# A two-block network step on one core: the conformer's layer-norm end one step later, and the turned ranks behind the LSTM's running sums

## The chip, the cores and the metric

The kernel runs on 1 core of one Trainium2 chip. The metric is the device time of one execution in microseconds; the time of a kernel is the median of its runs. A run is one launch that holds the whole computation. The profile is of one execution, and its times (us from the start of the span) come from the hardware profiler.

## The reference, cut to what matters

The model takes 256 tokens of width 1024 through a first block of two layers and a second block of one. Everything is float32.

```python
for l in range(2):                                  # first block
    proj = rms_norm(x, norm_g[l]) @ w_in[l]         # 1024 x 4376
    y_nsa  = sparse attention of q, k, v            # 8 heads of 64
    y_lru  = rg_lru(u_lru, ...)                     # gates, decay, scan over time
    u = ga * sigmoid(gb)                            # conformer branch
    u = depthwise conv of 31 taps (u)
    un = (u - mean(u)) * rsqrt(var(u) + eps) * ln_g + ln_b
    y_conv = silu(un) @ w_pw2                       # 512 x 512
    x = x + concat(y_nsa*silu(z), y_lru*silu(z), y_conv*silu(z)) @ w_out[l]
# second block: two mixers side by side, on 256 latent and 256 context tokens
cq  = rmsnorm(h @ w[:, 0:256],   g_cq)              # latent attention: ranks 256 and 128
ckv = rmsnorm(h @ w[:, 256:384], g_ckv)
q, k, v = cq @ w_uq, ckv @ w_ukv ...                # 4 heads, RMS-normed per head
i, f = gates;  F = cumsum(log_sigmoid(f));  M = cummax(i - F)   # mLSTM, both directions
x = x + gate * (concat(attention, mlstm) @ w_out)
x = x + gate * peer(h2)                             # 8 x 16 of 16384 experts for each token
```

## The kernel before, in words

The program is written out by hand, engine by engine. Each of TensorE (PE), VectorE (DVE), ScalarE (ACT), GpSimd (POOL) and SyncE (SP) has its own list of instructions and works through it strictly in order; semaphores named by events (`tell=...`, `at(...)`) tie the lists together. Matmuls write into PSUM banks. `take` hands them out in a fixed rotation, and TensorE waits there until the bank's previous content has been copied out (`taken`, `emptied`). SP loads weights, 2 MB at a time, into buffers that TensorE has finished with.

**First block, per layer.** After the projections a loop of 20 steps runs the attention. In each step TensorE makes scores of later heads, then what `BETWEEN` lists for that step, then turns (transposes) the weights of one head and multiplies them with the values. The steps around the change: in step 7 `BETWEEN` has `zn(1)`, a gate's projection; in step 8 `ada(0)`; in step 9 `mod(0)`, `pw(0)` and `pw(2)`, the two halves of the conformer's pointwise product; from step 10 on the output products `out12`. `pw` waits for the event `conv_act_ready`, which VectorE's `conv_act` gives (L1286). Ahead of that stand `layer_norm_end` (L1278: one multiply over 128x1024, four scale-and-add over 128x256, event `conv_normed`), and then on ScalarE the Tanh (L1531, event `conv_tanh`). `lru_scan` (L1248) and `lru_mixed` (L1259) are VectorE's work for the other branch; `lru_mixed` is first wanted in step 10. In VectorE's list the order is: scores of step 7, `layer_norm_end`, `z_nsa(1)`, `lru_scan`, `conv_act`, `lru_mixed`, scores of step 9.

**Second block, start ("head stage").** TensorE's list in `mix_tensor` (L1656): `mla` products, `conv_input` 4, 5, 0, 1, 2 (inputs of the mLSTM's convolution), the turns of `cq` and `ckv` (8 transposes into two banks, `cqT` and `ckvT`), `conv_input(3)`, the turns of the gates (`gate_i`, `gate_f`), the products `v(0)` and `v(1)`, a wait until VectorE has copied `ckvT` out, and then `queries(0)` (product `uq`), `v(2)`, `keys_values(0)` (`ukv`), and `heads_turned(0)`, which waits for `heads_normed`. After it six further rounds of `ukv` or `uq` products, turns of normed heads and a filling product follow.

VectorE's list in `mix_vector` (L1953): clear `qk_lat`, norm the ranks, `taken(0)` (copy `conv_input(0)` out), a polynomial for log(1+z) of the gates (event `log_gates_ready`), copy out `cqT` and `ckvT` with their gains (L2048 to L2053), `taken(1..3)`, four rounds of `silu` and `convolve`, copies of the gates, the running sums `sums(0)`, `sums(1)` up to the event `E_sum` (L2089), and then `head_norm(0)` (L2091). ScalarE's list (L2283 on): `values(0)`, `values(1)`, copies of `uq`, four squares (`head_squares`), then Exp of E, which waits for `E_sum`, then the square root for `head_norm(0)`.

**Rest.** After the head stage come attention and mLSTM of the first 128 tokens, their output product and the routing of the first expert head; from then on (about 706 us) GpSimd fetches expert rows of 8 KB, VectorE takes the dot products, TensorE sums them, and the other 128 tokens' mixers are fitted in between.

Of the kernel before, what the change touches and what calls it, by code (L numbers as in the profile page):

```python
# [252 lines left out]
class Banks:  # L253
# [32 lines left out]
    def filled(self, *key):  # L286
        return (f"bank{self.where(key)}_filled", *key)
# [736 lines left out]
def first_vector(c, m, block, K, x, l):  # L1024
# [261 lines left out]
    def conv_act():  # L1286
        dve.wait_ge(*at("conv_tanh", l))
        dve.stt(act, act, 1.0, conv, ADD, MUL, tell=("conv_act_ready", l))
# [18 lines left out]
    def between(step):  # L1307
# [4 lines left out]
        if step == 7:  # L1312
            layer_norm_end()
# [32 lines left out]
        if step == 8:  # L1346
            conv_act()
            lru_mixed()
# [37 lines left out]
def first_scalar(c, m, block, x, l):  # L1386
# [95 lines left out]
    def between(step):  # L1482
# [31 lines left out]
        if step == 4:  # L1514
            lru_decay()

    for step in range(STEPS):
# [11 lines left out]
        if step == 7:  # L1529
            act.wait_ge(*at("conv_normed", l))  # L1530
            act.f(m["conv_act"], conv, ACT.Tanh, scale=0.5, tell=("conv_tanh", l))  # L1531
# [124 lines left out]
def mix_tensor(c, m, K):  # L1656
# [48 lines left out]
    for o in range(3):  # L1705
        conv_input(o)
    pe.wait_ge(*at("ranks_normed", 0))
    bank = take("cqT")
    for k in range(2):
        for i in range(NT):  # L1710
            pe.turn(bank[:, k * T + i * P:k * T + i * P + P], m["cq"][:, i, k * P:k * P + P], ident,
                    tell=filled("cqT") if (k, i) == (1, NT - 1) else None)
    bank = take("ckvT")
    for i in range(TILES):
        pe.turn(bank[:, i * P:i * P + P], m["ckv"][:, i, 0:P], ident, tell=filled("ckvT") if i == TILES - 1 else None)
    conv_input(3)
# [9 lines left out]
    pe.wait_ge(*c.taken("ckvT"))  # L1726
# [226 lines left out]
def mix_vector(c, m, K, x):  # L1953
# [69 lines left out]
    dve.fill(qk_lat, 0.0)  # L2023
# [13 lines left out]
    taken(0)  # L2037
# [10 lines left out]
    dve.wait_ge(*full("cqT"))  # L2048
    for k in range(2):
        dve.ts(m["cqT"][:, k, :], tile("cqT")[:, k * T:k * T + T], vec[:, R_GCQ + k:R_GCQ + k + 1], MUL,  # L2050
               tell=emptied("cqT") if k else None)
    dve.wait_ge(*full("ckvT"))
    dve.ts(m["ckvT"], tile("ckvT")[:, :], vec[:, R_GKV:R_GKV + 1], MUL, tell=emptied("ckvT"))  # L2053
    for o in range(1, 4):
        taken(o)
    for o in range(4):
        silu((4, 5, 0, 1)[o])
        convolve(o)
# [30 lines left out]
    dve.tt(E, F, M, ADD, tell=("E_sum", 0))  # L2089

# [167 lines left out]
def mix_scalar(c, m, K, x):  # L2258
# [30 lines left out]
    values(1)  # L2289
    def product(n):  # L2290
# [17 lines left out]
    def head_norm(n):  # L2308
# [6 lines left out]
        if n == 0:  # L2315
            act.wait_ge(*at("E_sum", 0))
            act.f(m["E"], m["E"], ACT.Exp, scale=-1.0, tell=("E_ready", 0))
# [819 lines left out]
```

## Time and profile before

| | |
|---|---|
| time, median of 3 runs | 1426.55 us (1425.18 to 1427.67) |
| profiled execution: its own time | 1425.18 us |
| profiled execution: span | 1423.6 us, 1.6 us lie around it |
| TensorE busy | 1023.0 us, 72% |
| VectorE busy | 921.9 us, 65% |
| ScalarE busy | 357.7 us, 25% |
| mean granted TensorE clock | 0.842 of full speed |
| HBM read | 387.89 MB, 273 GB/s over the span |

Busy time is an average over stages with different limits: where one engine ends last in a stage, the others' busy share says nothing. In the rows further down, a number in square brackets is the time for which the engine was idle ahead of the instruction, with the engine and instruction that ended this.

### The profile page before, as it was taken

The numbers are of one execution on the slowest core, as the hardware profiler recorded it, in microseconds if no ns is written. First come the engines' busy times: TensorE is split into PE (matmuls) and PEld (weight loads), VectorE is DVE, ScalarE is ACT, GpSimd is POOL, SyncE is SP. The second block draws the span as 40 slices with busy tenths as digits, with TensorE's granted clock in tenths as the row PEclk, the third lists the DMA queues.
The fourth block names the chain that finished last, engine by engine and source line by source line (L and its number), as shares of the span: only waits on it lengthen the run. The fifth ranks groups of instructions, "written<-read, shape, count | busy, mean of one in ns | idle before, by whom it ended". The sixth has DMA issues, their size and how long they took to land.

```text
span 1423.6 us, 17219 instructions
## 1 busy us (share of the span) xinstructions
PE 1023.0 (72%) x6241; PEld 594.2 (42%) x6241; DVE 921.9 (65%) x2443; ACT 357.7 (25%) x813; POOL 288.0 (20%) x265
## 2 busy tenths in 40 slices
PE   7997999999899999978868668664543354543434
PEld 4776656577665556436534323332211122211111
DVE  5488633448864437544366788778777676777765
ACT  2013523101443412455244532321011110001100
POOL 0000000000000000000033334545433444433441
PEclk9998999999899899999979888976756666665765
DMA  8462562455456242162179899999999999999996
GB/s 295 150 193 98 187 220 89 162 178 165 144 182 222 63 144 96 59 239 90 34 290 412 327 420 418 418 414 419 415 421 415 419 414 416 417 414 414 420 421 274
DMA packets 111926, 391.10 MB, mean 275 GB/s; under 512 B 10971, under 2 KB 39182, under 8 KB 79586
## 3 DMA queue, kind: packets, MB, share of 16 engines
q0 software_dynamic: 37440, 268.45, 45.8%
q1 hardware_dynamic: 74402, 121.56, 24.7%
q8 instruction: 49, 0.80, 0.2%
q14 instruction: 35, 0.29, 0.1%
HBM read 387.89 MB, written 1.05 MB: 273 GB/s over the span
## 4 chain that ended last, share of the span: by engine, by line
DMA 21%; DVE 18%; PE 14%; ACT 4%; POOL 3%; issue 3%; DVEq 0%; ACTq 0%
DMA e_uv<-in_experts_dram,e_listed 21%; PE bank L169 13%; DVE e_uv L2814 5%; POOL e_uv L3021 3%; ACT m_W L229 1%; DVE e_rest L2745 1%; DVE e_diag L185 1%; ACT L229 1%; PE bank L174 1%; DVE e_hot L185 1%; DVE e_si L2743 1%; DVE e_si L2749 1%; DVE e_sv L2747 1%; DVE e_sv L2741 1%; DVE m_W L185 1%
## 5 line engine op out<-in xcount | busy, mean ns | idle before, releaser
L3021 POOL DMA_INDIRECT e_uv<-in_experts_dram,e_listed x252 | 278.9, 1107 | 1098.8 <-DVE e_listed L202 823.0
L169 PE MATMUL bank<-e_uv,e_diag 128*32 128x512 f32 x1024 | 232.1, 884 | 321.6 <-DVE e_diag L185 321.6
L2814 DVE CUSTOM_DVE_ANT_0 e_uv<-e_uv,e_h2q 128x1024 f32<-128x1024 f32 x192 | 229.3, 1221 | 84.5 <-DMA e_uv<-in_experts_dram,e_listed 84.1
L169 PEld LDWEIGHTS bank<-e_uv,e_diag 128*32 128x32 f32 x1024 | 41.5, 139 | 445.9 <-DVE e_diag L185 363.7
L169 PE MATMUL bank<-hT,weights 128*128 128x256 f32 x640 | 145.1, 388 | 2.7 <-DVE hT L191 1.4
L169 PEld LDWEIGHTS bank<-hT,weights 128*128 128x128 f32 x640 | 123.6, 195 | 22.3 <-issue 1.9
L229 ACT ACTIVATE e_act<-e_dot 128x4 f32<-128x4 f32 (+1 forms) x81 | 16.6, 205 | 394.7 <-DVE e_dot L2814 393.9
L229 ACT ACT_TABLE_LOAD x81 | 103.9, 1283 | 10.8 <-DVE e_dot L2814 2.8
L169 PE MATMUL bank<-weights,hT 128*128 128x512 f32 (+1 forms) x256 | 101.5, 552 | 2.2 <-DMA weights<-in_w_in_dram 2.2
L197 DVE SCALAR_TENSOR_TENSOR conv<-ubuf,vec,conv 128x256 f32<-128x256 f32 x240 | 96.8, 480 | 0.6
L2814 DVE CUSTOM_DVE_ANT_0 e_uv<-e_uv,e_hT 128x1024 f32<-128x1024 f32 x64 | 76.3, 1220 | 20.6 <-DMA e_uv<-in_experts_dram,e_listed 20.6
L169 PE MATMUL bank<-weights,mixT 128*128 128x512 f32 x192 | 87.5, 610 | 2.0 <-DVE mixT L202 1.6
L169 PEld LDWEIGHTS bank<-weights,hT 128*128 128x128 f32 x256 | 48.4, 192 | 49.1 <-issue 43.4
L169 PEld LDWEIGHTS bank<-e_hT,e_w_pq 128*128 128x128 f32 x512 | 63.8, 206 | 6.8 <-issue 6.0
L169 PE MATMUL bank<-e_hT,e_w_pq 128*128 128x128 f32 x512 | 65.4, 290 | 1.4 <-ACT e_hT L229 1.4
L169 PEld LDWEIGHTS bank<-weights,mixT 128*128 128x128 f32 x192 | 36.5, 196 | 46.3 <-issue 43.8
L185 DVE TENSOR_TENSOR x_sb<-bank,x_sb 128x512 f32<-128x512 f32 x16 | 11.1, 691 | 64.5 <-PE bank L169 64.5
L229 ACT ACTIVATE S<-S,mx 128x128 f32<-128x128 f32 (+1 forms) x64 | 29.1, 455 | 61.6 <-DVE mx L222 59.3
L169 PE MATMUL bank<-m_w,e_hT 128*128 128x464 f32 (+1 forms) x96 | 39.9, 570 | 1.2 <-PEq L3092 1.1
L185 DVE TENSOR_TENSOR e_w<-e_act,e_weight 128x4 f32<-128x4 f32 (+1 forms) x81 | 13.1, 162 | 30.9 <-ACT e_act L229 25.5
L197 DVE SCALAR_TENSOR_TENSOR ubuf<-fb,bank 128x512 f32<-128x512 f32 x4 | 2.7, 687 | 41.8 <-PE bank L169 41.8
L169 PE MATMUL bank<-m_wo,e_hT 128*128 128x512 f32 x64 | 28.2, 595 | 1.4 <-DVE m_qk_lat L202 1.4
(384 smaller groups left out, 1414.1 us busy)
## 6 DMA issues: line engine op xcount, KB each, us to landing
weights<-in_w_in_dram SPq DMA_DIRECT2D x16, 2048.0 KB, 8.1
weights<-in_w_ada_dram SPq DMA_DIRECT2D x8, 2048.0 KB, 8.7
weights<-in_w_out_dram SPq DMA_DIRECT2D x6, 2048.0 KB, 7.8
e_w_pq<-in_w_pq_dram SPq DMA_DIRECT2D x12, 1024.0 KB, 26.3
weights<-in_cmp_w_dram SPq DMA_DIRECT2D x4, 2048.0 KB, 8.4
m_w<-in_w_in_dram SPq DMA_DIRECT2D x2, 2048.0 KB, 8.1
m_wo<-in_w_ada_dram SPq DMA_DIRECT2D x2, 2048.0 KB, 8.4
m_w<-in_w_ada_dram SPq DMA_DIRECT2D x2, 2048.0 KB, 10.2
```

Of the source, the lines that this page charges most:

```text
L169: ins = self.engine.matmul(out, lhsT, rhs, start=start, stop=stop, **kw)
L174: ins = self.engine.transpose(out, a, ident)
L185: return self.mark(self.engine.tensor_tensor(out, a, b, op), tell)
L197: return self.mark(self.engine.scalar_tensor_tensor(out, a, s, b, op0, op1), tell)
L229: return self.mark(self.engine.activation(out, a, func, **kw), tell)
L2741: dve.mark(c.nc.vector.max(out_v[:, 0:8], values))
L2743: dve.mark(c.nc.vector.max_index(out_i[:, 0:8], out_v[:, 0:8], values))
L2745: dve.mark(c.nc.vector.match_replace(scratch, out_v[:, 0:8], values, -3e38))
L2747: dve.mark(c.nc.vector.max(out_v[:, 8:16], scratch))
L2749: return dve.mark(c.nc.vector.max_index(out_i[:, 8:16], out_v[:, 8:16], scratch))
L2814: dve.mark(c.nc.vector.tensor_tensor_reduce(u, u, h2q[tt][n], 1.0, 0.0, MUL, ADD, m["dot"][:, j:j + 1]), ("dots_set", g, c0) if n == c1 - ...
L3021: ins = c.nc.gpsimd.indirect_dma_start(out=to, out_offset=None, in_=rows, in_offset=bass.IndirectOffsetOnAxis(ap=of, axis=0))
```

## The change

It has two parts. In the first block, in both layers, `layer_norm_end` leaves step 7 and comes in step 8, behind `z_nsa(1)` and `lru_scan`; `lru_mixed` is put between it and `conv_act`; on ScalarE the Tanh moves from the end of step 7 into step 8, ahead of that step's copy of a turned head. In the second block the turns of `cq` and `ckv` move behind `v(1)` on TensorE and are spread over six banks instead of two; VectorE copies them out in eight pieces of 128x128 behind `E_sum`; the clearing of `qk_lat` and `taken(0)` move behind `log_gates_ready`, and the takings are interleaved with the convolutions; ScalarE makes Exp of E ahead of its first copy of `uq`.

```diff
--- before.py
+++ after.py
@@ -1309,8 +1309,6 @@
             conv_taps(*TAPS_AT[step])
         if step == 4:
             conv_taps(*TAPS_AT[step][0])
-        if step == 7:
-            layer_norm_end()
         for kind, *a in BETWEEN.get(step, ()):
             if kind == "zn":
                 z_nsa(*a)
@@ -1344,8 +1342,9 @@
         if step == 7:
             lru_scan()
         if step == 8:
+            layer_norm_end()
+            lru_mixed()
             conv_act()
-            lru_mixed()
 
     for step in range(STEPS):
         if step < len(UNITS):
@@ -1513,6 +1512,9 @@
                 modulation(*a)
         if step == 4:
             lru_decay()
+        if step == 8:
+            act.wait_ge(*at("conv_normed", l))
+            act.f(m["conv_act"], conv, ACT.Tanh, scale=0.5, tell=("conv_tanh", l))
 
     for step in range(STEPS):
         if step < len(UNITS):
@@ -1526,9 +1528,6 @@
         if 1 <= step <= len(UNITS):
             kind, qt, i, g = UNITS[step - 1]
             turned(step - 1, 2 * (qt + 1) * P if kind == "head" else P)
-        if step == 7:
-            act.wait_ge(*at("conv_normed", l))
-            act.f(m["conv_act"], conv, ACT.Tanh, scale=0.5, tell=("conv_tanh", l))
         if l + 1 < DEPTH and step == X_NORMED_AT:
             squares(l + 1, 0)
             root(l + 1, 0)
@@ -1702,18 +1701,8 @@
     conv_input(5)
     pe.wait_ge(*c.taken("blockT", "lat", NT - 1, 1))
     by_token("mla", TILES - 1, TILES - 1, B_QK + 16)
-    for o in range(3):
+    for o in range(4):
         conv_input(o)
-    pe.wait_ge(*at("ranks_normed", 0))
-    bank = take("cqT")
-    for k in range(2):
-        for i in range(NT):
-            pe.turn(bank[:, k * T + i * P:k * T + i * P + P], m["cq"][:, i, k * P:k * P + P], ident,
-                    tell=filled("cqT") if (k, i) == (1, NT - 1) else None)
-    bank = take("ckvT")
-    for i in range(TILES):
-        pe.turn(bank[:, i * P:i * P + P], m["ckv"][:, i, 0:P], ident, tell=filled("ckvT") if i == TILES - 1 else None)
-    conv_input(3)
     for a, name in enumerate(("gate_i", "gate_f")):
         bank = take(name)
         pe.wait_ge(*at("log_gates_ready", 0))
@@ -1723,7 +1712,16 @@
     by_token("v", 0, 0, 512)
     by_token("v", 1, 1, 512)
 
-    pe.wait_ge(*c.taken("ckvT"))
+    pe.wait_ge(*at("ranks_normed", 0))
+    for i in range(NT):
+        bank = take("cqT", i)
+        for k in range(2):
+            pe.turn(bank[:, k * P:k * P + P], m["cq"][:, i, k * P:k * P + P], ident,
+                    tell=filled("cqT", i) if k else None)
+    for i in range(TILES):
+        bank = take("ckvT", i)
+        pe.turn(bank[:, 0:P], m["ckv"][:, i, 0:P], ident, tell=filled("ckvT", i))
+    pe.wait_ge(*c.taken("ckvT", TILES - 1))
 
     def queries(i):
         view, landed = mix_weight(m, "uq")
@@ -2020,7 +2018,6 @@
     for name in ("M", "F"):
         dve.fill(m[name], 0.0)
 
-    dve.fill(qk_lat, 0.0)
     tmp = m["tmp"]
     f = gates[:, :, 8:16]
     dve.stt(tmp[:, 0], f, -1.0, f, MUL, MAX, tell=("gates_abs", 0))
@@ -2034,7 +2031,6 @@
             dve.ts(src[:, i, 0:width], src[:, i, 0:width], inv[:, i:i + 1], MUL,
                    tell=("ranks_normed", 0) if (name, i) == ("ckv", TILES - 1) else None)
 
-    taken(0)
     dve.wait_ge(*at("gates_exp", 0))
     log1p_unit(dve, tmp[:, 2], tmp[:, 1], tmp[:, 3], tmp[:, 4], tmp[:, 5])
     dve.ts(f, f, 0.0, MIN)
@@ -2045,15 +2041,9 @@
         dve.tt(both[1][:, :, of], f[:, :, d * ML_H:(d + 1) * ML_H], tmp[:, 2, :, d * ML_H:(d + 1) * ML_H], SUB,
                tell=("log_gates_ready", 0) if d else None)
 
-    dve.wait_ge(*full("cqT"))
-    for k in range(2):
-        dve.ts(m["cqT"][:, k, :], tile("cqT")[:, k * T:k * T + T], vec[:, R_GCQ + k:R_GCQ + k + 1], MUL,
-               tell=emptied("cqT") if k else None)
-    dve.wait_ge(*full("ckvT"))
-    dve.ts(m["ckvT"], tile("ckvT")[:, :], vec[:, R_GKV:R_GKV + 1], MUL, tell=emptied("ckvT"))
-    for o in range(1, 4):
+    dve.fill(qk_lat, 0.0)
+    for o in range(4):
         taken(o)
-    for o in range(4):
         silu((4, 5, 0, 1)[o])
         convolve(o)
     silu(2)
@@ -2087,6 +2077,16 @@
     sums(0)
     sums(1)
     dve.tt(E, F, M, ADD, tell=("E_sum", 0))
+
+    for i in range(NT):
+        dve.wait_ge(*full("cqT", i))
+        for k in range(2):
+            dve.ts(m["cqT"][:, k, i * P:i * P + P], tile("cqT", i)[:, k * P:k * P + P],
+                   vec[:, R_GCQ + k:R_GCQ + k + 1], MUL, tell=emptied("cqT", i) if k else None)
+    for i in range(TILES):
+        dve.wait_ge(*full("ckvT", i))
+        dve.ts(m["ckvT"][:, i * P:i * P + P], tile("ckvT", i)[:, 0:P], vec[:, R_GKV:R_GKV + 1], MUL,
+               tell=emptied("ckvT", i))
 
     def head_norm(n, g, rope_tile):
         heads, r1, r2 = m["both"][n % 2], m["r1"], m["r2"]
@@ -2287,6 +2287,9 @@
 
     values(0)
     values(1)
+    act.wait_ge(*at("E_sum", 0))
+    act.f(m["E"], m["E"], ACT.Exp, scale=-1.0, tell=("E_ready", 0))
+
     def product(n):
         kind, i, _ = HEAD_WORK[n]
         heads = m["both"][n % 2]
@@ -2312,9 +2315,6 @@
         for h in range(MLA_H):
             act.f(m["sq4"][:, h, :], heads[:, h, :], ACT.Square, accum_out=small[:, 24 + h:25 + h],
                   tell=("head_squares", n) if h == MLA_H - 1 else None)
-        if n == 0:
-            act.wait_ge(*at("E_sum", 0))
-            act.f(m["E"], m["E"], ACT.Exp, scale=-1.0, tell=("E_ready", 0))
         act.wait_ge(*at("head_inverse", n))
         act.f(small[:, 32:36], small[:, 28:32], ACT.Sqrt, tell=("head_root", n))
 
```

## Rows read from the trace of the kernel before

**Rows 1.** Windows: gather stage; us, then busy us (count) of PE, PEld, DVE, ACT, POOL, clock, DMA.

```profile
706.00:1423.00 717.00, 379.33 (x3344) 174.06 (x3343) 531.72 (x1396) 142.62 (x319) 287.75 (x261) 0.72 0.98 397
```

**Rows 2.** Timeline of PE, layer 0: start, us, what, count, [idle before].

```profile
174.40 1.05 PE L169 MATMUL bank<-constants,cond_mod_rows 128*128 128x2 f32 x8 [0.36 <-ACT cond_mod_rows L233]
176.22 7.14 PE L169 MATMUL bank<-xn,weights 128*128 128x256 f32 x32 [0.76 <-DVE xn L197]
```

**Rows 3.** Windows of PE alone, layer 0 from the pointwise product on.

```profile
176.20:234.00 57.80, 57.56 (x295) 1.00 0.55 191
```

**Rows 4.** Timeline of DVE, steps 7 and 8 of layer 0.

```profile
168.83 1.23 DVE L185 TENSOR_TENSOR conv<-conv,yt 128x1024 f32<-128x1024 f32 x1
170.09 1.38 DVE L192 TENSOR_SCALAR conv<-conv,vec 128x256 f32<-128x256 f32 x4
171.58 0.69 DVE L197 SCALAR_TENSOR_TENSOR zn<-zn,bank 128x512 f32<-128x512 f32 x1
172.30 2.44 DVE L218 TENSOR_TENSOR_SCAN fc<-fa,fd 128x256 f32<-128x256 f32 x4
174.85 1.23 DVE L197 SCALAR_TENSOR_TENSOR xn<-xn,conv 128x1024 f32<-128x1024 f32 x1
176.11 1.22 DVE L197 SCALAR_TENSOR_TENSOR mixT<-fb,fc 128x1024 f32<-128x1024 f32 x1
```

**Rows 5.** Timeline of ACT, layer 0: two Tanh.

```profile
169.44 0.60 ACT L229 ACTIVATE zn<-bank 128x512 f32<-128x512 f32 x1 [0.43 <-PE bank L169]
...
171.51 1.06 ACT L229 ACTIVATE xn<-conv 128x1024 f32<-128x1024 f32 x1 [1.10 <-DVE conv L192]
```

**Rows 6.** Timeline of PE, layer 1: the same pointwise product.

```profile
421.45 7.14 PE L169 MATMUL bank<-xn,weights 128*128 128x256 f32 x32 [0.76 <-DVE xn L197]
```

**Rows 7.** Timeline of PE, head stage.

```profile
551.97 1.04 PE L174 MATMUL bank<-constants,e_w_pq 128*128 128x128 f32 x8
...
559.31 14.00 PE L169 MATMUL bank<-m_wo,e_hT 128*128 128x512 f32 x32 [1.37 <-DVE m_qk_lat L202]
573.14 2.74 PE L169 MATMUL bank<-m_w,m_ctx 128*128 128x384 f32 x8
...
585.90 0.63 PE L174 MATMUL bank<-constants,e_w_pq 128*128 128x128 f32 x4 [1.43 <-DVE e_w_pq L185]
```

**Rows 8.** Timeline of DVE, head stage.

```profile
544.76 0.92 DVE L213 MEMSET m_qk_lat<- 128x1032 f32 x1 [0.16 <-issue]
...
549.04 1.25 DVE L191 TENSOR_SCALAR e_w_pq<-e_w_pq,m_small 128x128 f32<-128x128 f32 x4 [0.27 <-ACT m_small L229]
...
556.86 1.86 DVE L191 TENSOR_SCALAR m_ctx<-bank,cond_vec 128x256 f32<-128x256 f32 x3
...
578.89 0.68 DVE L185 TENSOR_TENSOR m_xn<-m_xn,m_M 36x512 f32<-36x512 f32 x1
...
581.85 0.96 DVE L185 TENSOR_TENSOR e_w_pq<-e_w_pq,m_small 128x768 f32<-128x768 f32 x1 [1.78 <-ACT m_small L229]
```

**Rows 9.** Timeline of ACT, head stage: last of the four squares, table load.

```profile
578.17 0.19 ACT L229 ACTIVATION_READ_ACCUMULATOR e_h2q<-e_w_pq 128x1 f32 x1
...
580.31 1.28 ACT L229 ACT_TABLE_LOAD   x1
```

**Rows 10.** Window of PE alone, head stage behind the first turned heads.

```profile
585.90:621.80 35.90, 35.90 (x138) 1.00 0.34 120
```

**Rows 11.** Timeline of PE, layer 0: one product behind a rest, and one without.

```profile
129.98 0.62 PE L169 MATMUL bank<-hidT,w 128*64 128x16 f32 x8 [3.70 <-DVE hidT L197]
130.73 8.95 PE L169 MATMUL bank<-hT,weights 128*128 128x256 f32 x32
...
140.53 7.12 PE L169 MATMUL bank<-hT,weights 128*128 128x256 f32 x32
```

**Rows 12.** Window of PE alone: the clock there.

```profile
130.00:134.40 4.40, 4.27 (x17) 0.50 0.00 2
```

**Rows 13.** Timeline of PE: the first levels of the first tile.

```profile
641.13 0.68 PE L169 MATMUL bank<-m_M,constants 36*128 36x128 f32 x4 [0.81 <-ACT cond_mod_rows L233]
```

## The prediction

> **What bounds the kernel now.** I read the page's forty slices first: from about 706 us on the DMA engines are full, before that they are not. The window over this gather stage [rows 1] shows it: DMA share 0.98, TensorE busy 379 of 717 us. Nothing of the change lies there, and its first transfer waits for the first routed expert list, the end of all that stands before. So I take the gather stage as a block that starts as much later as the work ahead of it ends later. Ahead of 706 us I asked, stretch by stretch, whether TensorE waits and for whom, with the timeline of one engine at a time. Behind the pointwise product of layer 0 it is busy 57.56 of 57.80 us [rows 3], behind the first turned heads of the head stage 35.90 of 35.90 [rows 10]. Whatever makes TensorE later at the start of such a stretch arrives whole at its end. At the two places that the change touches, TensorE already waits a little for VectorE: 0.76 us ahead of the pointwise product in each layer [rows 2, 6], 1.43 us ahead of the first turned heads [rows 7]. There VectorE's list is what ends last, and the change rewrites just this list.
>
> **Part 1, the layer-norm end, twice.** Before, VectorE does norm end, `z_nsa`, scan, `conv_act`, and the pointwise product starts 0.14 us behind `conv_act` [rows 2, 4]. The Tanh between norm end and `conv_act` (1.06 us [rows 5]) costs nothing: `z_nsa` and the scan (0.69 and 2.44 us [rows 4]) cover it. After, step by step:
> - The scores of step 7 end at 168.8 as before. `z_nsa` is now first and waits for its own Tanh, which ends at 170.04 [rows 5]. It runs from 170.1 to 170.8. Before, the norm end filled this hole; 1.3 us of it are now lost.
> - Scan, with its gaps, to 173.4.
> - Norm end: 168.83 to 171.55 before, 2.72 us with gaps [rows 4], so to 176.1.
> - Tanh on ScalarE 176.1 to 177.2. The cover is now `lru_mixed`, 1.22 us [rows 4], which ends at 177.35: it hides the Tanh, but it also stands ahead of `conv_act`.
> - `conv_act` from 177.4 to 178.6, where it ended at 176.08. That is **2.5 us later**: 1.3 for the hole and 1.22 for `lru_mixed`, which isn't wanted before step 10.
>
> What is queued behind: on TensorE `pw(0)`, `pw(2)`, the turned heads, the output products, all of one list, so the 2.5 us pass on. VectorE's scores of step 9 start 1.15 us later, at 178.65, and are done before the delayed product is. On ScalarE the copy of the turned head of step 8 now stands behind the Tanh, and ends near 177.7; its bank is next wanted by `pw(2)`, some 3.5 us behind 178.7, so this costs nothing (without that cover it would delay `pw(2)` by the remainder). Layer 1 shows the same row with the same wait [rows 6], so the term is 2 x 2.5 = 5.0 us.
>
> **Part 2, the ranks behind the running sums.** TensorE first gains. The 8 turns (1.04 us) and a wait of 1.37 us stand before `v(0)` [rows 7]; without them it starts 2.4 us earlier, at 556.9. It and `v(1)` take 14.00 us [rows 7], to 570.9, and the turns end near 571.8. Their six banks are free by then (the gates' copies end near 570, `v(0)`'s bank is copied near 568).
>
> Then TensorE waits for `taken("ckvT", 3)`, and what it waits for is now at the end of VectorE's sums:
> - `E_sum` ended at 579.57 [rows 8]. The three copies of the turned ranks ahead of it go (556.86 to 558.83, 1.97 us with gaps [rows 8]). The clearing (0.92 us [rows 8]) and `taken(0)` only change their place ahead of `E_sum`; I allow 0.2 us for that. `E_sum` comes at 577.8.
> - Eight pieces of 128x128 follow. Four of this shape took 1.25 us [rows 8], so eight take 2.5; the lower bound is the old 1.86 for the same columns in three pieces, the upper a third of those 1.86 us for each, 5.0. I take 2.5, from the row with the same shape. `queries(0)` starts at 580.4, not 573.14 [rows 7]: 7.3 us later, behind a rest of 8.6 us.
> - From there `uq`, `v(2)` and `ukv` take their 11.3 us. The 1.43 us wait for `heads_normed` [rows 7] vanishes if VectorE is in time: the squares ended at 578.36 [rows 9], hence now 585.7; a table load of 1.28 us [rows 9] and the root, 587.2; from 581.85 [rows 8] to the turned heads it was 3.95 us, hence 591.1. TensorE is there at 585.90 + 7.3 - 1.43 = 591.8. In time by 0.7 us, so 7.3 - 1.43 = 5.9 us pass on.
> - Four more `take`s shift the rotation of seven banks. The first `levels` then no longer gets the bank of `ada(11)`, for which it waited 0.81 us [rows 13]: -0.8 us.
> - Exp of E ahead of `uq` on ScalarE costs nothing: ScalarE waits there anyway.
>
> Term: 5.9 - 0.8 = 5.1 us.
>
> **The clock.** The change makes three rests of TensorE: twice 0.36 + 0.76 + 2.5 = 3.6 us ahead of the pointwise product (the wait of 0.36 us [rows 2] joins them, since `ada(0)` is copied earlier), and 8.6 us ahead of `queries(0)`. Behind a rest of 3.70 us the granted clock was 0.50 of full, that is 1.2 GHz instead of 2.4 [rows 11, 12], and a product took 8.95 us where its twin took 7.12 [rows 11]: 1.83 us. I charge this for each new rest, 5.5 us. Lower bound 0, if the slow spell falls into the rest; upper bound 3.7 each, twice the row. By the Trainium skill ("TensorE: Matmul & The Clock Gate", section "HAM oscillation — how this bites in real kernels") the extra time is half of the throttled time; for three spells like the 4.4 us of the window [rows 12] that would be 6.6 us where I have 5.5, and the forecast would be 1.1 us higher. The same section warns against just this kind of change, short bursts with rests between, and this case's rows agree (1.83 us lost behind 3.70 us).
>
> **Sum.** 5.0 + 5.1 + 5.5 = 15.6 us. The profiled execution took 1425.18 us itself (span 1423.6), so 1440.8; the median of the runs lies 1.4 above it: **1442.2 us**, +1.1%. A difference under 0.2% (2.9 us) can't be told from none for this kernel.
>
> **The rivals.**
> - *The clock charges nothing* (spells fall into the rests): +10.1, 1436.7. Against it: the rest of 3.70 us is about as long as the new ones, and it was charged.
> - *Layer part absorbed*: a transfer or a later wait ends last anyway, only part 2 counts, 5.1 + 1.8 = 6.9, 1433.5. Against it: 57.56 busy of 57.80 us [rows 3].
> - *A second new wait*: VectorE misses the turned heads, since the slow clock also delays `uq`; the margin is 0.7 us. Up to 3 us more: 1445.2.
> - *Part 2 is hidden*: VectorE copies the ranks before TensorE asks at 571.8. Then part 2 gives back 1.4 + 0.8 + up to 2.4 = 4.6 us, and part 1 costs 5.0: +0.4, near 1427, no change (1430.6 if the clock charges the layers' 3.7 us). It needs VectorE's list 6 us shorter than the rows say.
> - *Faster*: rest buys clock. The gather stage ran at a mean clock of 0.72 [rows 1], and at full clock its 379 us of TensorE work would be up to 106 us shorter (379 x 0.28). If rest ahead of it raised that clock and 21 us came back on the path, the result is 1421.2. It decides from 18.5 us on (15.6 and 2.9), a sixth of the 106. Against it: in rows 11 and 12 a rest is followed by the lower clock, not the higher, and the stage waits for DMA.
>
> **Numbers.** Likeliest 0.64 (own range 1438 to 1446), clock free 0.12, layer part absorbed 0.10, second wait 0.06, part 2 hidden 0.05, faster 0.03. Slower by over 0.2%: 0.92; within: 0.05; faster: 0.03. Slow spells in the gather stage can fall otherwise by a few us. For 8 in 10 the range goes from 1432, below the absorbed case, to 1449, with 3.7 us for each rest.
>
> **What the profile after would show.** In both layers the wait ahead of the `xn,weights` product is near 3.6 us instead of 0.76, and `conv_act` ends 2.5 us later against the scores of step 7. A rest near 9 us ahead of the 128x384 products, ended by VectorE's last piece; no wait ahead of the first turned heads; none ahead of the first `levels`. A granted clock of 0.5 behind each rest, with the products there about 1.8 us longer. The first gather near 722 instead of 706 us, and the gather stage of the same length. I am wrong if VectorE's `E_sum` comes before 574, if the pointwise wait stays under 2 us, or if the gather stage changes its length by more than 4 us.

## The result, and the profile after

The changed kernel takes 1448.04 us (median of 4 runs, 1445.53 to 1449.19) against 1427.11 us for the kernel before on the same chip (1425.18 to 1428.68): a ratio of 1.0144 [1.0130, 1.0158], 20.9 us slower. The forecast was 1442.2 us, slower than before, with a range from 1432 to 1449; its own range for the likeliest case, 1438 to 1446, was missed. One run of all that follow, of part 1 alone, took 3407.28 us and is left out of its ratio. The profiled execution of after took 1445.78 us, its span is 1444.5 us.

From the top of the profile page of after: TensorE's busy time rose by 13 us against the table above (1023.0 us), VectorE's by 1.5.

```profile
span 1444.5 us, 17228 instructions
PE 1035.9 (72%) x6241; PEld 601.4 (42%) x6241; DVE 923.4 (64%) x2448; ACT 357.7 (25%) x813; POOL 287.6 (20%) x265
```

TensorE, timeline, around the pointwise product of layers 0 and 1, which answer to [rows 2, 6]. The number in brackets is the idle time ahead of the instruction.

```profile
174.31 1.05 PE L169 MATMUL bank<-constants,cond_mod_rows 128*128 128x2 f32 x8
179.04 8.83 PE L169 MATMUL bank<-xn,weights 128*128 128x256 f32 x32 [3.68 <-DVE xn L197]
...
428.08 8.83 PE L169 MATMUL bank<-xn,weights 128*128 128x256 f32 x32 [3.68 <-DVE xn L197]
```

The wait grew from 0.76 to 3.68 us in both layers, with the old 0.36 us joined to it, so 2.56 us of it are new. The product itself takes 8.83 us where it took 7.14 [rows 2]. VectorE's list in the same place, which answers to [rows 4]:

```profile
170.40 0.69 DVE L197 SCALAR_TENSOR_TENSOR zn<-zn,bank 128x512 f32<-128x512 f32 x1 [1.33 <-ACT zn L229]
171.12 2.44 DVE L218 TENSOR_TENSOR_SCAN fc<-fa,fd 128x256 f32<-128x256 f32 x4
173.66 1.23 DVE L185 TENSOR_TENSOR conv<-conv,yt 128x1024 f32<-128x1024 f32 x1
174.92 1.38 DVE L192 TENSOR_SCALAR conv<-conv,vec 128x256 f32<-128x256 f32 x4
176.34 1.23 DVE L197 SCALAR_TENSOR_TENSOR mixT<-fb,fc 128x1024 f32<-128x1024 f32 x1
177.67 1.23 DVE L197 SCALAR_TENSOR_TENSOR xn<-xn,conv 128x1024 f32<-128x1024 f32 x1
```

The hole ahead of `z_nsa` is 1.33 us, as forecast. ScalarE's Tanh in its new place, and the copy queued behind it:

```profile
176.34 1.06 ACT L229 ACTIVATE xn<-conv 128x1024 f32<-128x1024 f32 x1 [3.60 <-DVE conv L192]
177.51 0.37 ACT L233 COPY PT<-bank 128x256 f32<-128x256 f32 x1
```

The head stage on TensorE, which answers to [rows 7]: the turns of the ranks now stand at 577.94, and behind them TensorE rests for 10.33 us. The first turned heads (602.05) have no wait ahead of them any more.

```profile
563.31 1.05 PE L174 MATMUL bank<-constants,e_diag 128*36 128x128 f32 x8
564.20 13.90 PE L169 MATMUL bank<-m_wo,e_hT 128*128 128x512 f32 x32
577.94 1.04 PE L174 MATMUL bank<-constants,e_w_pq 128*128 128x128 f32 x8
589.30 4.33 PE L169 MATMUL bank<-m_w,m_ctx 128*128 128x384 f32 x8 [10.33 <-DVE m_ctx L191]
593.46 7.03 PE L169 MATMUL bank<-m_wo,e_hT 128*128 128x512 f32 x16
600.33 1.88 PE L169 MATMUL bank<-m_w,m_ctx 128*128 128x512 f32 x4
602.05 0.60 PE L174 MATMUL bank<-constants,e_w_pq 128*128 128x128 f32 x4
...
657.92 0.71 PE L169 MATMUL bank<-m_M,constants 36*128 36x128 f32 x4
```

VectorE at the end of that rest, which answers to the `E_sum` row of [rows 8]: the last step of the running sums, then the eight pieces.

```profile
585.04 0.68 DVE L185 TENSOR_TENSOR m_xn<-m_xn,m_M 36x512 f32<-36x512 f32 x1
585.83 3.42 DVE L191 TENSOR_SCALAR m_ctx<-bank,cond_vec 128x128 f32<-128x128 f32 x8
```

TensorE in windows of after (length, then busy time and instructions, granted clock in parts of full, DMA share, GB/s): on the two pointwise products, behind the long rest, at two places behind 640 us, and over the gather stage [rows 1].

```profile
179.00:183.00 4.00, 3.96 (x11) 0.57 0.84 308
428.00:432.00 4.00, 3.92 (x11) 0.57 0.83 304
582.00:592.00 10.00, 2.70 (x4) 0.50 0.00 0
669.00:680.00 11.00, 9.61 (x30) 0.69 0.01 1
715.00:726.00 11.00, 8.82 (x42) 0.53 0.04 12
736.00:1443.00 707.00, 374.31 (x3082) 0.72 0.98 401
```

The kernel before has slow spells behind 640 us too. Counted from the first turned heads, the same two stretches of before had clocks of 1.00 and 0.75, where after has 0.69 and 0.53.

The first gather of expert rows on GpSimd, whose start in the trace of before is 719.91 us:

```profile
739.77 1.08 POOL L3021 DMA_INDIRECT e_uv<-in_experts_dram,e_listed  x1 [739.33 <-DVE e_listed L202]
```

**Where the 20.9 us come from.** Start of the same instruction in both traces, after minus before. "Own" is what the stretch up to there adds. Of the first 2.8 us, 0.3 were there already at 150 us, ahead of anything that the change touches.

| instruction | before | after minus before | own | forecast |
|---|---|---|---|---|
| pointwise product, layer 0 | 176.22 | 2.82 | 2.8 | 2.5 |
| first output product, layer 0 | 184.20 | 4.50 | 1.68 | 1.83 |
| first product of the hidden layer, layer 1 | 374.83 | 4.25 | -0.3 | 0 |
| pointwise product, layer 1 | 421.45 | 6.63 | 2.4 | 2.5 |
| first output product, layer 1 | 429.43 | 8.31 | 1.68 | 1.83 |
| `conv_input` 4 | 541.61 | 7.86 | -0.5 | 0 |
| `v(0)` | 559.31 | 4.89 | -2.97 | -2.4 |
| `queries(0)` | 573.14 | 16.16 | +8.3 from `conv_input` on | 7.3 |
| first turned heads | 585.90 | 16.15 | 8.29 from `conv_input` on | 7.7 |
| first `levels` | 641.13 | 16.79 | 0.6 | -0.8 |
| first gather | 719.91 | 19.86 | 3.1 | 0 |
| end of the span | 1423.6 | 20.9 | 1.0 | 0 |

Up to the first turned heads 16.15 us are lost where the steps gave 5.0 + 3.7 + 7.7 = 16.4. The other 4.7 us arise behind them, where the forecast had -0.8. Of these, 3.3 us arise within 17 us of the first `levels`, in four groups of matmuls that the change does not touch. Two neighbours among them, the second with 1.8 us the largest, in before and in after:

```profile
654.65 0.71 PE L169 MATMUL bank<-m_M,constants 36*128 36x128 f32 x4
655.29 1.98 PE L169 MATMUL bank<-m_knT,m_qnT 128*128 128x512 f32 x4
...
672.02 1.22 PE L169 MATMUL bank<-m_M,constants 36*128 36x128 f32 x4
673.17 3.78 PE L169 MATMUL bank<-m_knT,m_qnT 128*128 128x512 f32 x4
```

### The profile page after: what moved, and what is told of

The parts are those of the page before. It is cut to its first block, busy times and chain, and to the rows that moved or that the text cites. A ratio compares the mean times of both kernels' runs of the same rounds, so it can differ in the third digit from the quotient of the medians.

```text
span 1444.5 us, 17228 instructions
## 1 busy us (share of the span) xinstructions
PE 1035.9 (72%) x6241; PEld 601.4 (42%) x6241; DVE 923.4 (64%) x2448; ACT 357.7 (25%) x813; POOL 287.6 (20%) x265
## 4 chain that ended last, share of the span: by engine, by line
DMA 21%; DVE 18%; PE 15%; ACT 4%; POOL 3%; issue 3%; DVEq 0%; ACTq 0%
DMA e_uv<-in_experts_dram,e_listed 21%; PE bank L169 14%; DVE e_uv L2814 5%; POOL e_uv L3021 3%; ACT m_W L229 1%; DVE e_rest L2745 1%; DVE e_hot L185 1%; PE bank L174 1%; ACT L229 1%; DVE e_diag L185 1%; DVE e_si L2749 1%; DVE e_si L2743 1%; DVE m_W L185 1%; DVE e_sv L2747 1%; DVE e_sv L2741 1%
## 5 line engine op out<-in xcount | busy, mean ns | idle before, releaser
L169 PE MATMUL bank<-e_uv,e_diag 128*32 128x512 f32 x1024 | 235.6, 898 | 319.0 <-DVE e_diag L185 318.9
L229 ACT ACT_TABLE_LOAD x81 | 103.9, 1283 | 10.3 <-DVE e_dot L2814 2.2
L233 ACT COPY PT<-bank 128x256 f32<-128x256 f32 (+2 forms) x36 | 16.4, 455 | 55.3 <-PE bank L174 52.5
## 6 DMA issues: line engine op xcount, KB each, us to landing
m_w<-in_w_ada_dram SPq DMA_DIRECT2D x2, 2048.0 KB, 10.3
```

The lines of the kernel that those rows point to most:

```text
L169: ins = self.engine.matmul(out, lhsT, rhs, start=start, stop=stop, **kw)
L229: return self.mark(self.engine.activation(out, a, func, **kw), tell)
L233: return self.mark(self.engine.copy(out, a), tell)
```

## The experiments

Each kernel is compared with the kernel before within its own group of runs on one chip; between chips the time of the kernel before differed by up to 19 us, so only ratios and shifts inside one trace are carried from one group to another. Shifts are given against the trace of before. Three stretches are used: from `conv_input` 4 (541.61 in before) to the first turned heads; from these to the first gather (134.01 us in before); and from the start of the pointwise product to the first output product (7.98 us in before, of which 7.14 are the product).

### The two parts alone

Part 1 alone:

```diff
-        if step == 7:
-            layer_norm_end()
...
         if step == 8:
+            layer_norm_end()
+            lru_mixed()
             conv_act()
-            lru_mixed()
```

and the Tanh on ScalarE moved with it.

> Only the first part, the layer-norm end one step later, in both layers. My step: the pointwise product starts 2.5 us later in each layer and loses 1.7 us more to the half clock behind the rest, 2 x 4.2 = 8.4 us, some 1435.5. If the rests alone cost and the clock nothing: 5 us. If the remaining 4 to 5 us of the whole change, which the trace of the changed kernel shows behind 640 us, came from the shift of everything by the first part: 12 us or more.

Measured: ratio 1.0031 [1.0005, 1.0056]. The wait is 3.68 us in both layers, the first gather comes 10.47 us later. Of this 2.39 us were there already at 150 us, ahead of the first moved instruction (a second trace of the kernel before, below, has 2.37 there), so 8.1 us net. The head stage is as in before (conv_input to turned heads 0.00 longer). The trace confirms the step of 8.4 us. The ratio, on a chip whose runs of before spread over 17 us, gives 4.5 us, with an interval of 0.7 to 8.1, and so bears on the size only weakly.

Part 2 alone, that is, the changed kernel with those lines put back:

```diff
-    pe.wait_ge(*at("ranks_normed", 0))
-    bank = take("cqT")
...
+    for i in range(TILES):
+        bank = take("ckvT", i)
+        pe.turn(bank[:, 0:P], m["ckv"][:, i, 0:P], ident, tell=filled("ckvT", i))
```

> Only the second part, the turned ranks behind the running sums. By the trace of the changed kernel the first turned heads come 8.3 us later (7.3 forecast, 0.9 more for the eight pieces, 1.4 for the half clock, 1.43 of the old wait back). If the parts add up and the slow spells behind 640 us belong to this part: 12 us, 1439. If those spells are an accident of where they fall: 8 us, 1435, and then the two parts sum to less than the 21 us of the whole.

Measured: ratio 1.0105 [1.0069, 1.0140]. The rest is 10.33 us, and the stretch to the turned heads 9.12 us longer. It was run once more on a calmer chip:

> The second part alone once more. Its first trace took 133.1 us from the first turned heads to the first gather, the two traces of the whole change took 137.7, though all three run the same instructions there. If the difference is an accident of where the slow spells fall: this one lies between 133 and 138, and the three rests ahead are as before (0.76 in the layers, 10.3 in the head stage). If the first part caused it: 133.1 again, to within 0.5 us.

Measured: ratio 1.0077 [1.0063, 1.0092]; rest 10.32 us, stretch 8.51 us longer, and no slow spell on either pointwise product. From the turned heads to the first gather it took 132.6 us, 1.4 less than before (133.1 in the first run of this kernel, 0.9 less): 0.8 us of this are the bank wait that the forecast took off. Up to the first turned heads the parts add: 8.3 us with part 1 alone (10.66 later, less the 2.39), 8.5 to 9.1 with part 2 alone, and 15.8 with both (16.15 less 0.3). Most of the 1.0 to 1.6 us between the sum and the whole lies in how much the slow clock took: the product of layer 0 needed 9.34 us with part 1 alone and 8.83 in after, and from `queries(0)` to the turned heads the same products needed 12.75 us in after, 12.99 and 13.59 in the two traces of part 2 alone. Behind the turned heads the parts do not add.

### The changed kernel again, and the kernel before again

> The changed kernel once more, beside the kernel before on this chip. If the parts add up and the slow spells fall by accident: the three new rests of 3.68, 3.68 and 10.33 us are there again to within 0.1 us, the first turned heads come 8.3 us later against conv_input than before, and the start of the gather stage lies 14 to 20 us later than in one or the other trace of before. If the 4 us behind 640 us belong to the change: the distance from the first turned heads to the first gather is again 137.7 us where before has 134.0 and 134.0.

Measured: ratio 1.0177 [1.0152, 1.0203], more than the first 1.0144, on another chip. Rests of 3.68, 3.67 and 10.31 us, both pointwise products slow, conv_input to turned heads 8.28 us longer, turned heads to first gather 137.7 us: the numbers of the first trace of after came back, only the product of layer 0 took 9.17 us instead of 8.83.

> The kernel before once more, for a second trace. If the spells of half clock belong to the program: they lie at the same places (117, 128, 237, 363, 373, 479, 626, 636, 667 and 698 us), each within 1 us. If they depend on more than that: their number and length differ, and the start of the gather stage moves by some us, as much as the 4 us that my ledger does not explain.

Measured: 1443.33 us on a chip where the kernel before spreads from 1436.6 to 1453.7, and its first gather comes 3.44 us later than in the first trace: 2.4 us are there at 150 us, and most of the rest is a slow spell where there was none. Most of the longer time lies behind: from the first gather to the end of the span it took 718.5 us, where the first trace took 703.7. TensorE in the second trace of the kernel before, timeline and a window:

```profile
176.79 1.05 PE L169 MATMUL bank<-constants,cond_mod_rows 128*128 128x2 f32 x8 [0.37 <-ACT cond_mod_rows L233]
178.59 8.83 PE L169 MATMUL bank<-xn,weights 128*128 128x256 f32 x32 [0.75 <-DVE xn L197]
...
179.00:183.00 4.00, 4.00 (x13) 0.62 1.05 394
```

The waits are the old ones, 0.37 and 0.75 us, and yet the product takes 8.83 us at a clock of 0.62. The slow spell on the product is therefore not a sure mark of the longer wait. I counted it over all traces, by the stretch from pointwise product to output product. With a rest of 3.4 us or more right ahead (both layers of after, its second run, part 1 alone, and `lru_mixed` last, below) it was 1.68 to 2.19 us longer in 8 of 8. Without such a rest (the eight traces with the layers' old waits or shorter and nothing thrown away there, 16 places) it was longer in 3, and as long as before, within 0.03 us, in 13. So what happened in 3 of 16 places happened in 8 of 8 behind the rest, and the net charge is about 1.7 - 3/16 x 1.7 = 1.4 us for each place.

### Is it the rest, or what follows it?

The changed kernel, with products that are thrown away (128x256 each) in the rests, seven ahead of each pointwise product's wait and 22 ahead of the wait of `queries(0)`:

```diff
+        if ch == 0:
+            for _ in range(7):
+                pe.mm(bank[:, 0:T], K["ones"], hT[:, 0, :])
         pe.wait_ge(*at("conv_act_ready", l))
...
-    pe.wait_ge(*c.taken("ckvT", TILES - 1))
...
+            if (i, half) == (0, 0):
+                for _ in range(22):
+                    pe.mm(bank[:, 0:T], K["ones"], hTs[1][:, 0, :])
+                pe.wait_ge(*c.taken("ckvT", TILES - 1))
```

> The changed kernel, with extra matmuls that are thrown away in the three new rests (7 of 128x256 ahead of the pointwise product in each layer, 22 ahead of the first queries), so that TensorE stays busy while it waits; the waits themselves are unchanged. If the half clock behind the rests is a term of its own: 1.7 us less in each layer and 1.4 us in the head stage, 4.8 us less than the changed kernel, 1443. If the clock cost only moves, or the fillers delay the real work: no less than 1447. If the spells behind 640 us hang on the 10 us rest: up to 8 us less, 1440.

Measured: ratio 1.0086 [1.0057, 1.0115]. Compared with the 1.0144 of after on another chip this is more than the 4.8 us expected, which would give 1.0111, inside the interval; the size is read from the trace. The waits for VectorE end as late as ever, only filled. TensorE, timeline, and three windows of this kernel:

```profile
179.80 7.17 PE L169 MATMUL bank<-xn,weights 128*128 128x256 f32 x32 [0.46 <-DVE xn L197]
...
589.43 2.85 PE L169 MATMUL bank<-m_w,m_ctx 128*128 128x384 f32 x8 [0.75 <-DVE m_ctx L191]
...
180.00:184.00 4.00, 4.00 (x19) 1.00 0.79 292
428.00:432.00 4.00, 3.54 (x17) 1.00 1.02 376
582.00:592.00 10.00, 9.25 (x39) 1.00 0.01 2
```

The clock is 1.00 in all three places, where after had 0.57, 0.57 and 0.50. Pointwise product to output product takes 8.0 us in both layers instead of 9.66; `queries(0)` to the turned heads 11.27 instead of 12.75. That is 1.66 + 1.66 + 1.48 = 4.8 us, the clock's part of the loss up to 602 us, shown by taking it away with the waits left. What is not mended lies behind: turned heads to first gather took 137.5 us here too, so the slow clock behind the three rests does not cause the longer stretch there.

### What makes the layer's 2.5 us

Two orders. In the first `lru_mixed` goes behind `conv_act`, and the rest is as in part 1:

```diff
             layer_norm_end()
-            lru_mixed()
             conv_act()
+            lru_mixed()
```

> The first part alone, but with lru_mixed behind conv_act instead of ahead of it. My prediction put 1.22 us of the delay of conv_act down to lru_mixed. If so, the rest ahead of the pointwise product shrinks from 3.68 us to 2.5 us. The rival: the Tanh (1.06 us) stands there as well and needs its time in any case, so what counts is that the norm end came behind z_nsa and the scan, which had covered the Tanh: then the rest shrinks by 0.1 to 0.2 us only.

Measured: ratio 1.0042 [1.0015, 1.0070]. VectorE and TensorE of this kernel, timelines:

```profile
177.80 1.22 DVE L197 SCALAR_TENSOR_TENSOR xn<-xn,conv 128x1024 f32<-128x1024 f32 x1 [1.12 <-ACT xn L229]
...
179.17 9.25 PE L169 MATMUL bank<-xn,weights 128*128 128x256 f32 x32 [3.44 <-DVE xn L197]
```

The rest fell by 0.24 us only, from 3.68 to 3.44. Where `lru_mixed` stood, VectorE now waits 1.12 us for the Tanh. `lru_mixed` was not in the way; it filled a wait that the late norm end had opened.

In the second order the norm end goes back between `z_nsa` and the scan, so that the scan covers the Tanh again:

```diff
         if step == 7:
+            layer_norm_end()
             lru_scan()
         if step == 8:
-            layer_norm_end()
-            lru_mixed()
             conv_act()
+            lru_mixed()
```

> The first part, but the norm end stands between z_nsa and the scan, the Tanh of ScalarE at the end of step 7 as before, and conv_act ahead of lru_mixed. Then only the hole of 1.3 us is left, and the scan covers the Tanh: the pointwise product waits 2.1 to 2.4 us instead of 3.68 and 0.76, in both layers. If the hole were not the cause, it would be back at 0.8 to 1.1 us.

Measured: ratio 1.0014 [0.9989, 1.0040]. TensorE, timeline:

```profile
176.55 1.05 PE L169 MATMUL bank<-constants,cond_mod_rows 128*128 128x2 f32 x8 [2.38 <-ACT cond_mod_rows L233]
177.56 8.83 PE L169 MATMUL bank<-xn,weights 128*128 128x256 f32 x32
```

One rest of 2.38 us is left, and none ahead of the product. Against the old 0.36 + 0.76 this is 1.26 us more: the hole ahead of `z_nsa`, alone. It is ScalarE that ends the rest here, since its copy of `cond_mod_rows` is queued behind the Tanh. So the 2.56 us are 1.26 for the hole and 1.30 (3.68 - 2.38) for the Tanh, which the scan no longer covers. The product behind the rest of 2.38 us met a slow spell in layer 0 (8.83 us) and none in layer 1 (7.14 us).

### What makes the long rest

Part 2 alone, with the eight pieces between the two running sums:

```diff
     sums(0)
-    sums(1)
-    dve.tt(E, F, M, ADD, tell=("E_sum", 0))
     for i in range(NT):
         dve.wait_ge(*full("cqT", i))
...
     for i in range(TILES):
         dve.wait_ge(*full("ckvT", i))
         dve.ts(m["ckvT"][:, i * P:i * P + P], tile("ckvT", i)[:, 0:P], vec[:, R_GKV:R_GKV + 1], MUL,
                tell=emptied("ckvT", i))
+    sums(1)
+    dve.tt(E, F, M, ADD, tell=("E_sum", 0))
```

> The second part alone, with VectorE's eight copies of the ranks moved from behind E_sum to between the two directions of the running sums, 4.4 us earlier in its list. If the rest ahead of the first queries is set by the place of these copies: it is 5.9 us instead of 10.3. ScalarE's Exp of E, ahead of its copies of the first queries, then waits 3.4 us longer, and holds them up: the first turned heads come 3.5 to 4 us earlier than with the second part alone, not 4.4. If something else set the first queries' start: no change.

Measured: ratio 1.0032 [1.0010, 1.0054]. TensorE, timeline:

```profile
578.97 4.99 PE L169 MATMUL bank<-m_w,m_ctx 128*128 128x384 f32 x8 [5.91 <-DVE m_ctx L191]
...
592.74 0.63 PE L174 MATMUL bank<-constants,e_w_pq 128*128 128x128 f32 x4 [0.20 <-DVE e_w_pq L185]
```

The rest falls by 4.4 us and the stretch to the turned heads by 4.2 (4.89 longer than before, where part 2 had 9.12 in its first trace and 8.51 in its second). The place of the copies in VectorE's list sets the rest.

### Can both kernels be beaten?

The rows say how: VectorE's list ends last at both places, so shorten it. The kernel before, with the ranks copied by ScalarE ahead of the Tanh of `silu(0)`, and `conv_act` ahead of the scan:

```diff
         if step == 7:
+            conv_act()
             lru_scan()
         if step == 8:
-            conv_act()
             lru_mixed()
...
+            act.wait_ge(*full("cqT"))
+            for k in range(2):
+                act.f(m["cqT"][:, k, :], tile("cqT")[:, k * T:k * T + T], ACT.Copy, scale=vec[:, R_GCQ + k:R_GCQ + k + 1],
+                      tell=emptied("cqT") if k else None)
+            act.wait_ge(*full("ckvT"))
+            act.f(m["ckvT"], tile("ckvT")[:, :], ACT.Copy, scale=vec[:, R_GKV:R_GKV + 1], tell=emptied("ckvT"))
```

> The kernel before with two edits the other way: ScalarE, idle from 552 to 562 us, copies the turned ranks out instead of VectorE, and VectorE does conv_act ahead of the scan. If VectorE's list is what ends last at both places: the wait of 0.76 us goes in each layer (1.5 us), and up to 1.4 us of the waits of 1.37 and 1.43 us in the head stage: 3 us less than before, 1424. If TensorE's own list is what ends last: no change.

Measured: ratio 0.9988 [0.9962, 1.0013]. The wait of 0.76 us ahead of the pointwise product is gone in both layers, the 1.37 us ahead of `v(0)` are gone too, the 1.43 us ahead of the turned heads shrank to 1.10, and conv_input to turned heads is 1.96 us shorter. But turned heads to first gather took 135.5 us, 1.5 more than before, and the interval of the ratio does not tell the kernel from before. Then products that are thrown away were added at four places where TensorE rests before slow spells (`compressed_keys`, the turned heads of rounds 4 and 5, `att_turned` and the turns of `h2`):

```diff
+        for _ in range(7):
+            pe.mm(bank[:, 0:T], K["ones"], hT[:, 0, :])
         pe.wait_ge(*c.taken("cmp", l, 0))
...
+        for _ in range({4: 8, 5: 6}.get(n, 0)):
+            pe.mm(bank[:, 0:T], K["ones"], hTs[1][:, 0, :])
         pe.wait_ge(*at("heads_normed", n))
...
+        if (tt, h) == (0, 2):
+            for _ in range(8):
+                c.pe.mm(bank[:, 0:T], self.K["ones"], self.m["hT"][:, 0, :])
         c.pe.wait_ge(*c.taken("att_scores", tt, h))
...
+            if (tt, half) == (0, 0):
+                for _ in range(9):
+                    c.pe.mm(bank[:, 0:T], self.K["ones"], self.m["hT"][:, 0, :])
             c.pe.wait_ge(*c.at("h2_normed", tt))
```

> The kernel of e4 (ScalarE copies the ranks, conv_act ahead of the scan) with thrown-away matmuls in five old rests of TensorE of 3 to 4 us: 7 of 128x256 ahead of kcT in each layer, 8 and 6 ahead of the turned heads 4 and 5, 8 ahead of the third turned attention head, 9 ahead of the first h2 turns. If the half clock behind rests is a cost of its own: 1.5 to 2.8 us less at each of the six places, some 10 us, and with the 3 us of e4 the gather stage starts 10 to 13 us earlier than before, ratio 0.991. If the clock falls all the same, or the gather stage gives it back: no faster than before.

Measured: ratio 1.0050 [1.0030, 1.0069], a miss. TensorE, timeline, at the first of the four places:

```profile
126.76 0.42 PE L169 MATMUL bank<-kT,qT 64*128 64x128 f32 x4
130.87 5.99 PE L169 MATMUL bank<-hT,constants 128*128 128x256 f32 x14 [3.69 <-DVE hidT L197]
```

The rest of 3.69 us is still there, and the thrown-away products stand behind it: what TensorE waits for is the bank that `take` hands out, and they need that bank too. At `compressed_keys` (both layers) and at `att_turned` the wanted work started 5.9, 6.2 and 6.3 us later by them. Behind them it then ran at full clock (the product that took 8.95 us in before [rows 11] took 7.17), so that 3.5 to 3.7 us were lost at each place. At the heads and at `h2T`, where the bank is free, the stretches became 2.4 and 1.4 us shorter. With only those two places kept:

> As e10, without the three groups of extra matmuls that stood behind the wait instead of in it (7 in each layer, 8 ahead of the third turned attention head), which cost 6.4, 6.6 and 5.2 us in the trace of e10. What stays: 8 and 6 ahead of the turned heads 4 and 5, 9 ahead of the first h2 turns. From the first turned heads to the first levels e10 took 52.9 us where before took 55.2, and from the keys to the first gather 19.4 where before took 20.8. Added to e4 that is 4 us; with e4's 3 us the gather stage starts some 6 us earlier than before, ratio 0.996. If the fall of the spells decides more than the edits: between 0.995 and 1.003.

Measured: 1422.06 us (1421.29 to 1424.15) against 1428.51 (1426.06 to 1429.93), ratio 0.9959 [0.9946, 0.9973]: 0.4% faster than the kernel before, and so faster than both. How much of this the thrown-away products give beyond the shorter lists is not separated by the ratios, since this interval overlaps that of the shorter lists alone. In its trace conv_input to turned heads is 1.97 us shorter than in before, and turned heads to first `levels` 2.34 us shorter. From there to the first gather it took 78.8 us, as in before: the 1.4 us gained at `h2T` went to a slow spell, on the very two products that are slow in after.

```profile
650.88 1.22 PE L169 MATMUL bank<-m_M,constants 36*128 36x128 f32 x4
652.03 3.78 PE L169 MATMUL bank<-m_knT,m_qnT 128*128 128x512 f32 x4
```

## Why the prediction was right, and where it was not

**The total.** 1448.04 us lies inside the range, 1.0 us under its upper end, and 2 us outside the likeliest case's own range. That upper end stood for 3.7 us of clock at each rest, and that is not what happened: each rest cost about 1.7. The range held, in part, because room left for one cause took up another. The mechanism is right up to the first turned heads, and open behind them.

**The layers, 5.0 us: right in size, wrong in one cause.** The waits of 3.68 us are the 3.6 forecast, and the shifts 2.5 (2.8 less 0.3 from ahead of the change) and 2.4 us. The step that put 1.22 us on `lru_mixed` "also stands ahead of `conv_act`" failed: with `lru_mixed` moved away the rest lost 0.24 us. The text had both facts, that `lru_mixed` covers the Tanh and that it stands in the way, and charged the second. What costs is that the norm end stands behind the scan, so that the Tanh has no cover. The longer of the two things side by side decides, and they were nearly equal (an operation of 1.23 us, and a wait of 1.12 without it), so the size came out right by luck. The 1.3 us of the hole are confirmed by the second order (1.26).

**The head stage, 5.9 us without the clock: right, with two terms off.** `E_sum` comes at 585.72 us, less the 7.86 us of lateness at `conv_input`: 577.86, where 577.8 was forecast. The eight pieces were mis-sized: 3.42 us, not 2.5, 0.43 for each where the row of the same shape gave 0.31. It lies inside the bounds of 1.86 and 5.0. `v(0)` came 2.97 us earlier, not 2.4, since a wait of 0.45 us ahead of the turned gates went as well; this only lengthened the rest. So the rest is 10.33 us instead of 8.6, and `queries(0)` 8.3 us later instead of 7.3. No wait stands ahead of the turned heads, so 1.43 of it comes back, as said; the second new wait, a rival at 0.06, did not occur.

**The clock, 5.5 us: measured 4.8 up to the turned heads.** The two layers' 1.68 and the head stage's 1.48 are a little under the 1.83 charged (in the other traces behind such rests it was 1.68 to 2.19 in the layers and up to 2.32 in the head stage). The rival in which the clock charges nothing is out (8 of 8 places in the layers, and the filled rests), but the kernel before sometimes pays as well, which the forecast did not think of. By the Trainium skill ("TensorE: Matmul & The Clock Gate", section "HAM oscillation — how this bites in real kernels") the extra time is half of the throttled time. The window at 179 agrees: 4 us at a mean clock of 0.57, between the two levels 0.5 and 1.0, hold 3.4 us of half clock, and 1.68 us were lost.

**The bank wait, -0.8 us: right by itself, then eaten.** The wait ahead of the first `levels` is gone. With part 2 alone the stretch from turned heads to `levels` is 0.7 to 0.9 us shorter (three traces); in after it is 0.6 longer.

**Nothing behind that: wrong by 3 to 4 us.** That the gather stage "starts as much later as the work ahead of it ends later" held for the gather stage (1.0 us more at its end), but the forecast carried the delay unchanged from 602 to 740 us. Its ground, that TensorE is busy there, covers only the first 36 us [rows 10]. The stretch from turned heads to first gather took 137.7, 137.7 and 137.5 us in three traces that have both parts, against 134.0 in both traces of before, 133.8 with part 1 alone, and 132.6 to 133.1 with part 2 alone. The slow spells fall otherwise, on work that the change does not touch, and with waits ahead that did not grow (1.99 us where before had 1.98, ahead of the slow pair of products). They do not need the two parts: the kernel with the shorter lists, which has neither, took 135.5 us, the one with the norm end between `z_nsa` and the scan 134.9, and the last kernel has the same slow pair as after. Nor is it the time since the start of the span alone: the turned heads came at 603.93 us in the second trace of after and at 603.97 in the first of part 2 alone, and 137.7 and 133.1 us followed. Why both parts together gave 137.5 to 137.7 in three of three traces stays open. It is the size of most of the miss (5.8 us in the median).

**The rest of the rivals.** The absorbed layer part is out: part 1 alone moved the first gather by 8.1 us net. Part 2 hidden is out by 10.33 us of rest. "Rest buys clock" is out: the gather stage ran at a clock of 0.72 as before [rows 1] and took 704.7 us from its first gather on, where it took 703.7. One number of the prediction was loosely put: the first gather stood at 719.91 us, not 706, in the trace of before; 706 is where its forerunners begin. The forecast is 735.5 for it and 739.77 was measured.

## What to carry to other kernels

Before an instruction is moved later in a list because its result is not wanted yet, look at what it filled and at what the moved chain covered: here two waits of 1.1 to 1.3 us, each hidden by ordinary work before, came into the open. The rests that such a move opened on TensorE were paid a second time by the clock behind them, 1.5 to 2.3 us for rests of 3.4 to 10.3 us. Slow spells also fell otherwise on work that the change never touched: the stretch from turned heads to first gather took 132.6 to 137.7 us in kernels that have the same products there. So a sum made at the change's own place carries an uncertainty of some us that no row at that place shows. Products thrown away in a rest brought the clock back only where they did not themselves need what ends the rest, a bank above all.

## What the runs showed of the hardware that was not expected

- The same product, in the same kernel with the same waits of 0.37 and 0.75 us ahead of it, took 7.14 us in one execution and 8.83 in another: a slow spell can fall there by accident. One trace of before does not show which spells belong to it.
- Eight scale-and-copy instructions of 128x128 from PSUM took 0.43 us each. The four from SBUF in [rows 8] took 0.31. The source alone does not explain it, since eight of the same shape from PSUM, with two operands, took 2.63 us together at 540.45 us of after, 0.33 each. What does was not measured.
- The kernel before differed between chips by 19 us in the median (1427.1 to 1446.1), and on the two slowest its runs spread over 17 us, so that the ratios there are uncertain by 0.2 to 0.35% either way, and smaller effects were read from traces. In the two traces of before the difference lies mostly in the gather stage: 703.7 us at 403 GB/s from the first gather on, and 718.5 us at 395 GB/s.
